# A two-block transformer kernel in fp32 on one core: layer norms by token tile, and the second feed-forward matrix stream by stream

## The reference, cut to what matters

```python
# first block, for l in range(2)
h = x * (1 + scale1) + shift1
y = token_mixer(h, ...)                                   # ends with y @ w_out
x = layer_norm(ALPHA * x + gate1 * y, ln1_g[l], ln1_b[l])
h = x * (1 + scale2) + shift2
y = moe_ffn(h, ...)                                       # 64 experts, top 8, and a shared one
x = layer_norm(ALPHA * x + gate2 * y, ln2_g[l], ln2_b[l])
...
# second block: layer 0 attention, layer 1 RWKV; x are the tokens, xc the context
h = rmsnorm(x, norm1_g[i]) * (1.0 + sc1) + sh1            # hc the same of xc
y, yc = attention_mixer(...) if i == 0 else rwkv_mixer(...)
x = x + gt1 * y
x = x + gt2 * (square(relu(n(x) @ w1)) @ w2)              # the feed-forward part
if i == 0:                                                # the context has one in layer 0 alone
    xc = xc + cgt1 * yc
    xc = xc + cgt2 * (square(relu(n(xc) @ w1)) @ w2)
...
# rwkv_features starts with a shift over the sequence and six mixtures of it
xx = 0.5 * (hp[:, :-2] + hp[:, 2:]) - h
xr, xw, xk, xv, xa, xg = [h + xx * mu[m] for m in range(6)]
k = heads(xk @ w_rkv[1])
```

## Time and profile before

| | |
|---|---|
| median of 3 runs | 3740.5 us (3738.17 to 3747.9) |
| the profiled execution, its own time | 3740.32 us |
| its span, from first to last instruction | 3738.4 us |
| PE busy | 3350.6 us, 90% of the span |
| DVE busy | 1212.5 us, 32% |
| ACT busy | 649.7 us, 17% |
| POOL busy | 215.9 us, 6% |
| DMA, mean over the span | 184 GB/s |
| granted clock of TensorE, mean | 0.958 |

### The profile page before, as it was taken

One profiled execution on the slowest core, in us unless ns is written; L12 is line 12 of the kernel. 1 busy time (PEld: TensorE's weight loads), 2 busy tenths in 40 slices (PEclk: granted clock), 3 DMA queues, 4 the chain that ended last, 5 costly groups with the idle time before them and its releaser, 6 DMA issues. The chain is left out here.

```text
span 3738.4 us, 67774 instructions
## 1 busy us (share of the span) xinstructions
PE 3350.6 (90%) x29432; PEld 2358.1 (63%) x29432; DVE 1212.5 (32%) x2347; ACT 649.7 (17%) x1254; POOL 215.9 (6%) x186
## 2 busy tenths in 40 slices
PE   7997899999887889989979999999988889887899
PEld 5776466566666556556557664444457877776788
DVE  1334232233333423323245442100054454444200
ACT  0111011111120111111123221000022313332100
POOL 0000000000000000000000000000004410341000
PEclk9998999999999899999989999999999999998899
DMA  7655398899473559969912351222221013100342
GB/s 278 222 209 204 153 398 334 347 404 395 153 272 124 202 229 408 393 276 401 378 39 98 140 181 68 74 73 79 79 95 48 4 34 124 37 4 3 125 157 102
DMA packets 113862, 686.22 MB, mean 184 GB/s; under 512 B 11040, under 2 KB 11216, under 8 KB 49504
## 3 DMA queue, kind: packets, MB, share of 16 engines
q1 hardware_dynamic: 109920, 668.69, 46.2%
q0 software_dynamic: 3584, 12.25, 1.0%
HBM read 679.85 MB, written 1.05 MB: 182 GB/s over the span
## 5 line engine op out<-in xcount | busy, mean ns | idle before, releaser
L204 PE MATMUL ps<-arena 128*128 128x256 f32 (+2 forms) x2432 | 630.4, 422 | 45.1 <-issue 17.5
L204 PEld LDWEIGHTS ps<-arena 128*128 128x128 f32 (+1 forms) x2432 | 471.5, 195 | 197.9 <-issue 123.3
L120 ACT ACTIVATE arena<-ps 128x512 f32<-128x512 f32 (+1 forms) x526 | 265.5, 505 | 1541.2 <-PE ps L204 374.7
L1089 PE MATMUL ps<-arena 128*64 128x256 f32 x4096 | 480.9, 385 | 29.7 <-issue 29.6
L1089 PEld LDWEIGHTS ps<-arena 128*64 128x64 f32 x4096 | 317.3, 139 | 190.7 <-issue 81.6
L2114 PE MATMUL ps<-arena 64*64 64x64 f32 x10496 | 306.0, 224 | 60.0 <-issue 23.1
L1481 PE MATMUL ps<-arena 128*128 128x512 f32 (+1 forms) x1024 | 336.3, 492 | 10.0 <-DVE arena L146 10.0
L2114 PEld LDWEIGHTS ps<-arena 64*64 64x64 f32 x10496 | 292.1, 139 | 74.6 <-issue 40.1
L1493 PE MATMUL ps<-arena 128*128 128x512 f32 (+1 forms) x1024 | 330.6, 486 | 0.0
L137 DVE TENSOR_TENSOR arena<-arena,ps 128x512 f32<-128x512 f32 (+1 forms) x276 | 163.1, 591 | 461.7 <-PE ps L2114 240.0
L1481 PEld LDWEIGHTS ps<-arena 128*128 128x128 f32 x1024 | 197.3, 193 | 148.6 <-issue 132.9
(11 more groups left out here) (189 smaller groups left out, 2558.7 us busy)
## 6 DMA issues: line engine op xcount, KB each, us to landing
arena<-in_w_gate SPq DMA_DIRECT2D x128, 1024.0 KB, 8.9
arena<-in_w_up SPq DMA_DIRECT2D x128, 1024.0 KB, 12.2
arena<-in_w_down SPq DMA_DIRECT2D x128, 1024.0 KB, 8.9
arena<-in_mlp SPq DMA_DIRECT2D x64, 1024.0 KB, 4.7
arena<-in_w_ada SPq DMA_DIRECT2D x48, 1024.0 KB, 7.2
arena<-in_ada SPq DMA_DIRECT2D x48, 1024.0 KB, 4.8
arena<-in_w_in SPq DMA_DIRECT2D x30, 1024.0 KB, 6.3
arena<-in_w_rkv SPq DMA_DIRECT2D x20, 1024.0 KB, 4.9
```

What stands on the lines that cost most here:

```text
L120: self.e.activation(out, in_, func, bias=bias, scale=scale, **more).then_inc(*self.done(key))
L204: ins = pe.matmul(out, a, b, start=start and i == 0, stop=stop and i == len(pairs) - 1)
L1089: ins = pe.matmul(psum.of["gu", l, new][64 * ab:64 * ab + 64, i_ * 256:i_ * 256 + 256], xe[:, k, new % 2 * 128 + 64 * ab:new % 2 * 128 + 6 ...
```

## The change

1. In the first block, `mixer_pe` runs over t outside and i inside for `w_out`; DVE adds `ALPHA * XS` by 256 columns, takes statistics by halves, and normalises tile 0 while PE works on tile 1. `ln_dve` gives way to `ln_half`, `ln_stats` and `ln_rest` for one tile each, with two fused instructions (subtract and multiply, multiply and add) in the place of one per tile and two on both tiles. The square root on ACT is one for each tile. The end of `moe` does the same by halves of 512 columns.
2. `turned_pe` transposes tile 0 as soon as it is normalised, then tile 1.
3. The pumps of the `moe` rounds run two rounds earlier, and the last `pump.until` at p = 30.
4. The second matrix of the feed-forward part of layer 0 runs for the context (s = 1) over all eight blocks, then for the tokens (s = 0), each with matmuls of 256 columns; its 16 pieces are loaded twice. `h1` is laid out stream by stream.
5. After the context's blocks DVE does the context's norm, shift and first four mixtures (`context_dve`); PE's `eighths_pe` for it stands after the tokens' block 0.

```diff
-        def turned_pe(pe, l, which):
+        def turned_pe(pe, l, which, ready):
...
-                for kk in range(2):
-                    for t in range(2):
+            for t in range(2):
+                reach(pe, *at[ready(t)])
+                for k2 in range(4):
+                    for kk in range(2):
                         c = kk * 256 + t * 128
...
+        def ln_half(do, t, i, h):
+
+            do.bns(LN[0][:, i, h, :], t[:, i * 1024 + h * 512:i * 1024 + h * 512 + 512])
+
+        def ln_stats(do, key, i):
+            do.bna(LN[1][:, i, :], LN[0][:, i, :, :], ("ln stats", key, i))
+
+        def ln_rest(dve, do, key, t, g, bvec, dst, i):
+
+            f = slice(i * 1024, i * 1024 + 1024)
+            do.stt(t[:, f], t[:, f], LN[1][:, i, 0:1], g, ALU.subtract, ALU.mult)
+            dve.wait_ge(*at["ln root", key, i])
+            do.rcp(LN[2][:, i:i + 1], LN[2][:, i:i + 1])
+            do.stt(dst[:, f], t[:, f], LN[2][:, i:i + 1], bvec, ALU.mult, ALU.add, ("ln", key, i))
...
-            for i in range(4):
-                w = weights.of["w_out", l, i].rearrange("p (k c) -> p k c", k=8)
-                reach(pe, *at["w_out", l, i])
-                for t in range(2):
+            for t in range(2):
+                for i in range(4):
+                    w = weights.of["w_out", l, i].rearrange("p (k c) -> p k c", k=8)
+                    reach(pe, *at["w_out", l, i])
...
-                yield p, p + 1 if p < 31 else None, Q, ks, (p + 1) * NPUMP[l] // 32 - max(p, 0) * NPUMP[l] // 32
+                n = [min(max(i, 0), 32) * NPUMP[l] // 32 for i in (p + 2, p + 3)]
+                yield p, p + 1 if p < 31 else None, Q, ks, n[1] - n[0] if p >= 0 else n[1]
...
+            dve.wait_ge(*at["moe", l])
+            dve.wait_ge(*at["added", l, 31, 0])
+            gated(0, 0)
             dve.wait_ge(*at["added", l, 31, 1])
+            gated(0, 1)
+            ln_stats(do, ("moe", l), 0)
+            gated(1, 0)
+            gated(1, 1)
+            ln_stats(do, ("moe", l), 1)
             for t in range(2):
...
+                ln_rest(dve, do, ("moe", l), E.hT, E.lg, E.lb, XS[:, :], t)
...
-            for mt in range(8):
-                for hf in range(2):
-                    load(sp, ("mlp2", l, mt, hf), ("mlp", l, mt, hf), D["mlp2"][l, mt, hf])
+            for s in MLP[l].last:
+                for mt in range(8):
+                    for hf in range(2):
+                        load(sp, ("mlp2", l, s, mt, hf), ("mlp", l, s, mt, hf), D["mlp2"][l, mt, hf])
...
-                        ins = pe.matmul(b[:, 0:W], w[:, k, :], m.h1[:, kk, :], start=kk == 0, stop=kk == 31)
-                    ins.then_inc(*made(("mlp", l, mt, hf)))
...
+                            ins = pe.matmul(b[:, 0:256], w[:, k, :], m.h1[:, kk, s, :], start=kk == 0, stop=kk == 31)
+                        ins.then_inc(*made(("mlp", l, s, mt, hf)))
+                    if (l, s, mt) == (0, 0, 0):
+                        eighths_pe(pe, ("scan", 1), [1], R)
...
+                if s:
+                    context_dve(dve, pump, do)
...
+            eighths_dve(dve, do, ("scan", 1), 1, 0, [1], R)
+            dve.wait_ge(*at[("scan", 1), "normed", 1, 7])
+            shift_dve(do, 1)
+            mixtures(do, 1)
```

More of the change, by code:

```diff
@@ L999, in moe_sp @@
                     pump()
-            pump.until(0, l, 5)
+                if p == 30:
+                    pump.until(0, l, 5)
             weights.size = NRING
@@ L1338, in moe_dve, with gated @@
                     pump()
[L1339 removed]
+                if p == 30:
+                    pump.until(0, l, 5)
             av = E.hT.rearrange("p (t n) -> p t n", t=2)
[L1341 to L1348 removed]
+            def gated(t, nh):
+                do.tt(av[:, t, nh * 512:nh * 512 + 512], psum.tiles[ACC + t * 2 + nh][:, :],
+                      gate[1][:, nh * 512:nh * 512 + 512], ALU.mult, ("sum out", l, t * 2 + nh))
+                z, x = (v[:, t * 1024 + nh * 512:t * 1024 + nh * 512 + 512] for v in (E.hT, XS))
+                do.stt(z, x, ALPHA, z, ALU.mult, ALU.add)
+                ln_half(do, E.hT, t, nh)
+            dve.wait_ge(*at["moe", l])
+            dve.wait_ge(*at["added", l, 31, 0])
+            gated(0, 0)
+            dve.wait_ge(*at["added", l, 31, 1])
+            gated(0, 1)
[3 more added lines that the diff above has]
+            ln_stats(do, ("moe", l), 1)
+            for t in range(2):
+                ln_rest(dve, do, ("moe", l), E.hT, E.lg, E.lb, XS[:, :], t)
             end(("moe", l), "dve", formed)
@@ L1830, in features_pe @@
                 pump.until(1, 1, 0, 1, 2)
-                eighths_pe(pe, ("scan", 1), [1], R)
             def wide(m, src):
@@ L2001, in shift_dve, with mix, mixtures, context_dve @@
             do.stt(xx, xx, 0.5, h, ALU.mult, ALU.subtract, ("shifted", s))
+        def mix(do, s, m, dst):
+            mu = vec(f"mu{m}")
+            m = {0: 0, 1: 3, 2: 1, 3: 2, 4: 4, 5: 5}[m]
+            for k in range(8):
+                do.stt(dst[:, k, :], R.shift[s][:, k, :], mu[:, k:k + 1], R.h[:, k, :], ALU.mult, ALU.add, ("mix", s, m, k))
+        def mixtures(do, s):
+            for m, dst in zip((2, 4, 1, 3), R.mixed):
+                mix(do, s, m, dst)
+        def context_dve(dve, pump, do):
+            do.ts(R.kvec, vec("k_a"), -1.0, 1.0, ALU.mult, ALU.add)
+            for d in range(2):
+                do.ms(R.Z[d], 0.0, ("z", "start", d))
+            do.ms(scanm, 1.0)
+            do.ms(scanm.rearrange("p (c t) -> p c t", t=64)[:, :, 0:1], 0.0)
+            pump.until(1, 1, 0, 1, 2)
+            eighths_dve(dve, do, ("scan", 1), 1, 0, [1], R)
+            dve.wait_ge(*at[("scan", 1), "normed", 1, 7])
+            shift_dve(do, 1)
+            mixtures(do, 1)
         def features_dve(dve, pump, s, before):
```

132 lines of the change are left out of this document (51 added, 81 removed).

## The result

| | median us | runs | ratio to the kernel before |
|---|---|---|---|
| before | 3738.17 | 3737.98 to 3747.9 | |
| change | 3719.95 | 3715.78 to 3729.34 | 0.9945 [0.9928, 0.9961] |
| change, second series (before there: 3744.85) | 3721.81 | 3711.31 to 3729.21 | 0.9933 [0.9916, 0.9949] |

The change is faster, by 21 us (15 to 27) in the first series and 25 in the second. I had forecast 37.4 us and a range from 3694 to 3715 us: a little more than half the gain came, and the time lies above the range. The profiled execution of the change took 3724.46 us (span 3722.7), 4.5 above its median.

A forecast was written before the change was run, and what follows sets the result against it. PE, busy for 90% of the span, was taken to bound the kernel. Gains of 19.2 + 3.6 + 1.0 − 0.5 + 14.1 = 37.4 us off 3740.3 gave 3703 us, range 3694 to 3715.

The forecast's parts named there:

- After E 4.8 + 3.7 = 8.5 us instead of 18.1: Mixers' layer norms: from last `w_out` product's end to router's product, 4.8 us DVE's rest plus 3.7 us transposes and scaling.
- 9.6 us each: Mixers' layer norms: gain per mixer from the shorter wait, 19.2 us for two, bounds 7 and 10.5 each.
- The clock comes back too: Rival at the layer norms: shorter waits no longer drop the clock, 4 us more gain, 3699 us; chance 0.07.
- End of layer 0's moe: Wait from last addition to next mixer's product falls from 22.8 to 17.5 us; gain 3.6 us net of the pump.
- PE still pays for it, 1.7 us: Layer 0's moe: the last pump, moved to round 29, still costs PE 1.7 us there.
- costs 2.2: End of layer 1's moe: the pump moved ahead of the last addition costs 2.2 us; the term's gain is 1.0 us.
- Second matrix, +1.5 us: Layer 0's feed-forward part: 1024 records of 256 columns take 221.4 us instead of 219.9 for 512 of 512 columns.
- the weight load's rival: Second matrix: loads no longer hide beneath shorter matmuls, 406 ns a record, 3897 us in all; chance 0.01.
- Context's norm, shift and mixtures, "14.1 us": Ahead of `wide`: 12.9 us wait goes, 2.7 us from full clock, less 1.5 for the split matrix; bounds 11 and 16.
- First mixer, −0.5 us: First mixer: the new transpose order completes its first bank later, a loss of 0.5 us, bounds −1.4 and 0.
- the rivals of the tiles and the features: Mixers' tiles do not overlap, 3714 us, chance 0.05; features gain nothing since something else delays the scan, 3718.5, chance 0.05.
- the rival without a gain in the features: Scan's start hangs on something ending as late as `wide` did; only layer norms gain, 3718.5 us; chance 0.05.

The follow-up runs named there:

- fill_best: fill_mix plus 16 dummy products ahead of the first selection of tokens in each experts' part; 3703.67 us, 0.9894 of the kernel before.
- best_pumps_back: fill_best with the pumps placed as in the kernel before and dummy counts adjusted behind layer 0's experts; 3704.29 us, 0.9884 of the kernel before.
- before_fill: The kernel before, with 50 and 9 dummy products in the long waits at both mixers' ends; 3742.98 us, 0.9995 of the kernel before.
- fill_mix: The change with dummy products covering PE's waits at both mixers' ends and behind layer 0's experts; 3702.14 us, 0.9891 of the kernel before.

## Why the prediction was wrong

- **"After E 4.8 + 3.7 = 8.5 us instead of 18.1"**: right, 8.7 us. The chain of DVE came out to 0.1 us. (Its term for eight transposes, "8 × 3.68 / 16", was read from a row at the low level; they took 1.97 us because they stood at that level again.) What failed is the step from this to the gain, "9.6 us each": it prices the wait and leaves the work behind it at its old pace. From the router on that work took 3.0 and 2.4 us longer than in the first profile of before, 1.5 us a layer over all profiles.
- **The failed step is the rival "The clock comes back too".** I took from the earlier trace rows that long waits drop the clock, and asked only whether shorter ones would spare it. I gave a gain of 4 us a chance of 0.07, and a loss none. The runs show the other sign: a wait of 4 us, or 2 + 2 with a microsecond of work between, still drops it, and the low stretch then lies on the products. Low work from the router to the first expert's second product was 12.4, 12.4, 12.8 and 17.2 us in the two executions of before, and 17.5 to 18.0 in all four places of the change. Over the whole kernel low work rose by 25 us, 12.5 us of time. Dummy products in these waits took 18 us off the change. A bound was due here that lets the low level lie on all work behind the wait.
- **End of layer 0's moe, "3.6 us"**: the wait went as calculated (22.8 to 17.8, forecast 17.5), but the mixer behind it and its router's stage gained 4.7 us instead of 9.6, with 8 us more of low work.
- **The pumps, "PE still pays for it, 1.7 us" and "costs 2.2"**: mis-sized. In layer 1 the products and waits alone were 4.0 us; by fill_best and best_pumps_back the rounds paid all that the ends gained, 6.9 us where I had charged 3.9. Together the rounds lost 10.9 us against my sum: 3 of them are the pumps' by this pair, 7.4 are low work, of which it stays open how much the change brings and how much is the executions' spread.
- **Second matrix, +1.5 us, and the weight load's rival**: right. 332.0 us and no idle time ahead of any of its 1536 records.
- **Context's norm, shift and mixtures, "14.1 us"**: right. `wide` follows the tokens' last product without idle time and runs at full clock:

```profile
2724.66 8.80 PE L1518 MATMUL ps<-arena 128*128 128x256 f32 x40
2733.30 27.79 PE L1855 MATMUL ps<-arena 128*128 128x256 f32 x128
```

  From the feed-forward part's first product to the end of `wide` it took 14.8 us less on average. Here the clock was on my side, because the wait was removed and not shortened: `wide` had 4.3 and 5.7 us of low work before and has none now. The further 3.6 us that the last stage gave lie behind `wide`, where the two executions of before differ by 4 us; nothing here explains them.
- **First mixer, −0.5 us, the rivals of the tiles and the features**: the tiles do overlap, the features did gain, and the first mixer's term is smaller than its stage's spread. That 3720 us lies next to the 3718.5 of the rival without a gain in the features is chance: its mechanism did not occur.
- **The range** failed for the same reason: nearly all its bounds were of waits, and the clock moved by more than most of them. It was also cut at 3715 us, although the lower bounds of the terms added up to 3718; the measured time lies beyond both.

## What to carry to other kernels

Where the engine that bounds the kernel waits, look at its granted clock behind the wait as well as at the wait. In this kernel the wait that was removed gave its time and the clock; the waits that were cut from 13 us to 4 gave the difference, less 1.5 to 3 us each for the work that the low level now lies on. Price that by the window behind the wait, and where it matters put harmless work into what remains of the wait: here 83 dummy products at three places were worth 18 us, nearly as much as the change. Keep them out of blocks that branches skip, where they cost 32 us here. And where a comparison is of 20 us in 3740, take a second profile of both kernels before an effect is put down to the change.

## What the hardware showed unexpectedly

- The clock fell behind waits of 2.05 us in the rounds and behind two of 2 us at the mixer's end, not only behind the long ones. It does not do so each time: in before_fill a wait of 2.0 us ahead of the transposes was followed by the low level in layer 0 and not in layer 1.
- With the same code and nearly the same waits, low work differs between executions (212 and 235 us before, 254 and 244 in the change), and so does where a low stretch ends: behind the same wait of 13 us, 10.4 us of work in two pieces or 14.9 in one. By halves these differences are 5 to 11 us, a good part of the 14 and 18 us over which the change's two series of times go.
- PE's busy time less half its low work is nearly the same in the two executions of each kernel, 3244.0 to 3244.6 us, while the busy time itself goes from 3350.6 to 3370.9.
- Dummy products hold the clock at 1.00 over what were waits of 4 and 11 us, in fill_mix at no cost that shows; in before_fill the gain in place did not arrive in the whole time.
- Instructions added to a block that is skipped cost time on the path that skips it: waits on PE's sequencer there went from 0.5 us in all to 22.6. The bytes of the queue that loads instructions hardly changed (4.77 and 4.96 MB). What takes the time there is open.
